# An encoder block in three stages: one program, expert lists of 128 slots, lists made on ScalarE, and another order of ScalarE's step

## The chip, the cores and the metric

The kernel runs on one core of one Trainium2 chip. The metric is the device time of one execution in microseconds, given as the median of several. The change is measured against the kernel before in the same way.

## The reference, cut to what matters

The block takes 512 rows (tokens) of 1024 float32 values:

```python
h = layer_norm(x)
# mixing: projections, spatial gating, stick-breaking attention, two gated branches
merged = sigmoid(gate_a) * (yA @ w_branch_a) + sigmoid(gate_b) * (yB @ w_branch_b)
h = layer_norm(ALPHA * h + merged @ w_out)
# experts: sigmoid scores, 4 of 8 groups, 8 of 64 experts per token
r = ALPHA * h + sum over the 8 picked experts e of
        weight[e] * ((silu(h @ gate[e]) * (h @ up[e])) @ down[e])      # 1024 -> 256 -> 1024
      + (silu(h @ sh_gate) * (h @ sh_up)) @ sh_down                    # one shared expert
r = r + sigmoid(r @ ple_w_gate) * (p @ ple_w_proj)
out = layer_norm(r)
```

Each of the 64 experts sees 64 tokens in the mean (512 x 8 / 64). The weights of one expert are 3 MB: gate, up and down with 1 MB each.

## The kernel before

It is written instruction by instruction, with semaphores. Every float32 product is made of three products of parts: an operand is split into a high part (ScalarE rounds it to the type fp32r) and a low part (VectorE subtracts the high part from the whole), and `product3` (L400 to L402) multiplies high by high, low by high and high by low.

Three functions, each with a Block of its own, follow each other; between two Blocks all engines meet. `mix_block` makes everything up to the merged rows. `out_block` multiplies them with `w_out` (weight pieces 22 to 25 of a ring with two raw buffers and four split ones), normalises the rows, stores them to `h1`, turns them, and begins the shared expert (`gate_up(0)`). `experts_block` makes the router's scores (`score`, `turn_scores`), picks the experts (`pick`, `weigh`), gives each pair of token and expert a slot in the expert's list (`count`, `place`), finishes the shared expert (`gate_up`, `turn_h`, `down`, `add_rows`, `store_rows`), and runs a loop over the 64 experts. At last `Embedding` makes the per-layer input and the last norm.

A list has `SLOTS` = 96 places. No expert has more tokens here, so one round over the experts is enough; a second would run if one had more. `one_hot` compares the slot numbers (`slots`, laid out by one iota in 16 groups of 6) with the tokens' slots (L1663); `locate` multiplies that with tags (L1480); `find` sums them to token number and weight, and makes the list for the gather (L1671, L1676). An unused place gets a number beyond the last token, and the transfer skips it. GpSimd gathers the rows from `h1` by an indirect transfer (`gather`, L1791) and adds the results to one of two tensors in memory, even and odd experts apart (`scatter`, L1803, an indirect transfer with addition).

In the loop, the step of expert x is written out for each engine:

- SyncE: load down(x); load gate and up of x+2, each as soon as VectorE has made the low part that frees its buffer.
- TensorE: turn the hidden rows of x-1 (L1513), locate x+4, gate and up of x (24 matmuls), turn the gathered rows of x+1 (L1489, 8 matmuls), down of x-1 (12 matmuls).
- ScalarE: high part of the hidden rows of x-1 (L1599); high parts of gate and up of x+1 (L1580); silu of x (L1595); high part of the gathered rows of x+1 (L1590); high part of down x (L1586); scaling of the result rows of x-1 (L1605).
- VectorE: low part of the hidden rows of x-1 (L1709); low part of gate of x+1 (L1688); find x+4; one-hot x+5; low part of up of x+1; product with up (L1704); low part of the gathered rows of x+1 (L1698); low part of down x (L1693); list for the scatter of x (`put_list`, L1682, two buffers).
- GpSimd: gather x+4, scatter x-1.

Of the kernel before, what the change touches and what calls it, by code (L numbers as in the profile page):

```python
# [12 lines left out]

# [3 lines left out]
P = 128  # L17
# [15 lines left out]
SLOTS = 96  # L33
FAR = 4096.0
QUEUES = 16
# [13 lines left out]
KB = 1024  # L49


class Memory:


    def __init__(self, nc, base, cap):
# [48 lines left out]
        self.peak_i = at("peak_i", [P, 1], I32, 206)  # L104

# [24 lines left out]
        self.put_idx = [at(f"put_idx{i}", [P, 1], U32, 180.75 + i * 0.0625) for i in range(2)]  # L130
# [11 lines left out]
        self.hT_lo = at("hT_lo", [P, 2, 2 * cap], F32R, 181)  # L142
        self.y = [at(f"y{i}", [P, D], F32, 102 + 4 * i) for i in range(2)]
        self.onehot = at("onehot", [P, 2, NT, cap], BF16, 182.5)
# [10 lines left out]
def set_constants(nc, m, pool, base_set, constants_set, cap):  # L155
# [8 lines left out]
    pool.wait_ge(base_set, 7)  # L164
    for eye in (m.ident, m.ident_bf):
# [12 lines left out]
    nc.gpsimd.iota(m.slots[:, 0:rounds * cap].rearrange("p (r q j) -> p r q j", r=rounds, q=QUEUES),  # L178
                   pattern=[[cap, rounds], [1, QUEUES], [QUEUES, cap // QUEUES]], base=0, channel_multiplier=0,
                   allow_small_or_imprecise_dtypes=True)  # L180
# [306 lines left out]
def mix_block(nc, m, ps, norm_semaphores, a, h0, ring, merged_turn, CAP):  # L487
# [8 lines left out]
    with ExitStack() as ctx:  # L496
        def sem(name):
            return ctx.enter_context(nc.semaphore(f"mix_{name}"))

        half_used, projected, gelu_out, copied = sem("half_used"), sem("projected"), sem("gelu_out"), sem("copied")  # L500
        small_in = sem("small_in")
        sg_turned, sg_w_ready = sem("sg_turned"), sem("sg_w_ready")
        v_moments, v_rooted = sem("v_moments"), sem("v_rooted")
        v_stats, v_scaled, v_normed = sem("v_stats"), sem("v_scaled"), sem("v_normed")
        gated, ya_ready = sem("gated"), sem("ya_ready")
        ya_turned, ya_hi, ya_lo = sem("ya_turned"), sem("ya_hi"), sem("ya_lo")
        z_ready, sig_ready, a_ready = sem("z_ready"), sem("sig_ready"), sem("a_ready")
        a_turned, aT_ready, av_done = sem("a_turned"), sem("aT_ready"), sem("av_done")
        yb_hi, yb_lo = sem("yb_hi"), sem("yb_lo")
        gate_sum, branch_sum, gate_ready, merged = sem("gate_sum"), sem("branch_sum"), sem("gate_ready"), sem("merged")  # L510
        chain, base_set, constants_set = sem("chain"), sem("base_set"), sem("constants_set")
        norm = RowNorm(nc, m, ps, norm_semaphores, banks=(3, 5))
        for c in range(5):
            ring.freed[2 * c], ring.freed[2 * c + 1] = (half_used, c + 1), (projected, 4 * c + 4)
        for j in range(4):
            ring.freed[10 + 3 * j] = (half_used, 5 + j + 1)
            ring.freed[11 + 3 * j], ring.freed[12 + 3 * j] = (gate_sum, 4 * j + 4), (branch_sum, 4 * j + 4)
        block = ctx.enter_context(nc.Block())
# [3 lines left out]
        SPLIT_AFTER_PAIR = {6: (14,), 7: (15,), 8: (16,), 14: (17,), 15: (18, 19)}  # L522
        SPLIT_AFTER_GATE = {10: (20,), 11: (21,), 12: (22,)}

        LAST_BEFORE_H0 = DENSE_PIECES - 6

        def width(s):
            return (s // HEADS + 1) * P

        def block_done(p):  # L530

            qb, last = divmod(p - 3, 4)
            return qb if p >= 3 and last == 3 else None

        def unit_bank(u):
            return FIRST_UNITS[u] if u < len(FIRST_UNITS) else MAIN[u % 2]

        @block.sync
        def _(sp):
            def load_rows(t):  # L540
                sp.dma_start(m.x[:, t], a["x"][0][t * P:(t + 1) * P, :]).then_inc(norm_semaphores.rows_in[t], 16)

            load_rows(0)
            norm.load_affine(sp, a["ln_in_g"], a["ln_in_b"])
            load_rows(1)
            ring.load(sp, 0)
            ring.load(sp, 1)
            load_rows(2)
            load_rows(3)
            sp.dma_start(m.sg_w[:], a["sg_w_s"][0].rearrange("g i j -> i g j")).then_inc(small_in, 16)  # L550
            norm.store(sp, 0, h0)
            norm.store(sp, 1, h0)
            ring.load(sp, 2)
            ring.load(sp, 3)
            sp.dma_start(m.sg_g[:], a["sg_ln_g"][0].partition_broadcast(P)).then_inc(small_in, 16)
            sp.dma_start(m.sg_bb[:], a["sg_ln_b"][0].partition_broadcast(P)).then_inc(small_in, 16)
            sp.dma_start(m.sg_b[:], a["sg_b_s"][0].rearrange("g i -> i g"),
                         allow_slow_non_contiguous=True).then_inc(small_in, 16)
            norm.store(sp, 2, h0)
            norm.store(sp, 3, h0)  # L560
            for i in range(4, DENSE_PIECES):
                ring.load(sp, i)
                if i == LAST_BEFORE_H0:
                    norm.stored(sp)
                    sp.wait_ge(branch_sum, 8)
                    for t in range(NT):
                        sp.dma_start(m.x[:, t], h0[t * P:(t + 1) * P, :]).then_inc(merged_turn.rows_in, 16)

        @block.gpsimd
        def _(pool):  # L570
            set_constants(nc, m, pool, base_set, constants_set, CAP)

        @block.tensor
        def _(pe):
            def unit_start(u):

                if u < 4:
                    return
                if u < 6:
                    pe.wait_ge(gelu_out, u - 3)  # L580
                elif u - 2 >= 8:
                    pe.wait_ge(copied, u - 2 - 8 + 1)
                else:
                    pe.wait_ge(gelu_out, u - 2 + 1)

            def rows_unit(u, c, t, between=None):

                unit_start(u)
                for half in range(2):
                    i = 2 * c + half  # L590
                    if t == 0:
                        ring.ready(pe, i)
                    for k in range(4):
                        kk = 4 * half + k
                        last = product3(nc, ps[:, unit_bank(u)], m.act_hi[:, kk, t * P:(t + 1) * P],
                                        m.act_lo[:, kk, t * P:(t + 1) * P], ring.hi(i)[:, k], ring.lo(i)[:, k],
                                        kk == 0, kk == KD - 1)
                    if half == 0 and t == NT - 1:
                        last.then_inc(half_used, 1)
                    if half == 0 and between is not None:  # L600
                        norm.turn(pe, between)
                last.then_inc(projected, 1)

            def features_unit(u, c, f):

                unit_start(u)
# [64 lines left out]
            def gate_part(g, part):  # L671
# [18 lines left out]
                if part < 3:  # L690
                    return
# [1391 lines left out]
```

## Time and profile before

| | us |
|---|---|
| median of 3 runs | 1160.66 |
| lowest, highest | 1159.36, 1161.66 |
| the profiled execution | 1162.54 |
| its span, first to last instruction | 1160.7 |

A reader of the rows below should know: PE is TensorE's matmuls, PEld its weight loads, DVE is VectorE, ACT is ScalarE, POOL is GpSimd and SP is SyncE. A row of a stretch has the start and end, its length, busy us of PE, PEld, DVE, ACT and POOL with the number of instructions, the granted clock as a share of full speed, the mean share of the 16 transfer engines that was busy, and what they moved. A group has a line, an engine, an operation, output and inputs with shapes and its count; then busy time in us and mean ns of one, then idle time before it and what ended that. Since matmuls overlap, the start of one to the start of the next is their pace, not their duration.

### The profile page before, as it was taken

What the parts mean: (1) busy time and instruction counts of PE and PEld (TensorE: products, weight loads), DVE (VectorE), ACT (ScalarE), POOL (GpSimd) and SP (SyncE); (2) the same over time, 40 slices, a digit from 0 to 9 for tenths busy, and PEclk for the clock granted to TensorE, in tenths of its full rate; (3) what the DMA queues carried; (4) which work ended last, traced back from release to release, by engine and by line L of the source; (5) the groups of instructions that cost most, each with busy time, mean ns of one, the idle gap of its engine ahead of it and who ended that gap; (6) DMA issues with size and microseconds to landing.
All of it is one profiled execution on the core that took longest, in us unless ns stands there. A gap on an engine that the chain in (4) does not pass through costs nothing.

```text
span 1160.7 us, 15673 instructions
## 1 busy us (share of the span) xinstructions
PE 1098.8 (95%) x5374; PEld 821.6 (71%) x5374; DVE 842.4 (73%) x1030; ACT 682.2 (59%) x689; POOL 316.6 (27%) x179
## 2 busy tenths in 40 slices
PE   4999999999999889999999999999999999999796
PEld 3878776668878557777777776767777777677475
DVE  6644437453356567999999988989889989887376
ACT  3332325351223326888888878778778878777253
POOL 1000000000004423444444434424334433231431
PEclk9999999989999899999999999999999999999898
DMA  8522213023256357999999999999999999997821
GB/s 316 179 76 73 88 58 109 1 83 121 87 191 235 127 215 257 355 368 370 371 370 363 369 361 368 364 356 363 360 363 365 368 362 364 361 355 248 272 91 55
DMA packets 68477, 294.79 MB, mean 254 GB/s; under 512 B 11217, under 2 KB 14289, under 8 KB 43601
## 3 DMA queue, kind: packets, MB, share of 16 engines
q1 hardware_dynamic: 52944, 256.43, 58.6%
q0 software_dynamic: 14912, 35.68, 12.5%
q10 hardware_dynamic: 576, 2.10, 0.5%
q8 instruction: 27, 0.44, 0.2%
q14 instruction: 18, 0.14, 0.0%
HBM read 275.29 MB, written 35.65 MB: 268 GB/s over the span
## 4 chain that ended last, share of the span: by engine, by line
PE 40%; DMA 14%; DVE 6%; issue 3%; ACT 3%; ACTq 0%; DVEq 0%; SPq 0%
PE ps L400 11%; PE ps L402 11%; PE ps L401 11%; DMA gu_raw<-in_moe_w_up 10%; DMA gu_raw<-in_moe_w_gate 4%; PE ps L1489 3%; ACT w_hi L1580 2%; DVE w_lo L1688 2%; PE ps L1943 1%; PE ps L1229 1%; PE ps L1513 1%; PE ps L1480 1%; DVE w_lo L384 1%; DVE grp L1297 0%; PE ps L1924 0%
## 5 line engine op out<-in xcount | busy, mean ns | idle before, releaser
L1688 DVE TENSOR_TENSOR w_lo<-gu_raw,w_hi 128x2048 fp32r<-128x2048 f32 x126 | 288.4, 2290 | 53.1 <-ACT w_hi L1580 53.0
L1580 ACT ACTIVATE w_hi<-gu_raw 128x2048 fp32r<-128x2048 f32 x128 | 242.6, 1913 | 52.7 <-DMA gu_raw<-in_moe_w_up 39.5
L400 PE MATMUL ps<-w_hi,xgT_hi 128*96 128x512 f32 x512 | 205.8, 402 | 5.7 <-issue 3.2
L1791 POOL DMA_INDIRECT xg<-h_rows,get_idx x64 | 154.3, 2410 | 204.9 <-DVE get_idx L1676 162.2
L402 PE MATMUL ps<-w_hi,xgT_lo 128*96 128x512 f32 x512 | 203.1, 397 | 0.0
L401 PE MATMUL ps<-w_lo,xgT_hi 128*96 128x512 f32 x512 | 201.6, 394 | 0.0
L400 PE MATMUL ps<-w_hi,act_hi 128*128 128x512 f32 x384 | 154.9, 404 | 6.1 <-PEq L496 2.8
L402 PE MATMUL ps<-w_hi,act_lo 128*128 128x512 f32 x384 | 150.9, 393 | 0.0
L401 PE MATMUL ps<-w_lo,act_hi 128*128 128x512 f32 x384 | 150.9, 393 | 0.0
L1693 DVE TENSOR_TENSOR dn_lo<-dn_raw,dn_hi 128x2048 fp32r<-128x2048 f32 x64 | 146.1, 2283 | 5.5 <-ACT dn_hi L1586 5.0
L1586 ACT ACTIVATE dn_hi<-dn_raw 128x2048 fp32r<-128x2048 f32 x64 | 122.2, 1910 | 12.9 <-issue 8.5
L279 POOL TENSOR_TENSOR x_rows<-x_rows,ln_b 128x1024 f32<-128x1024 f32 x6 | 14.4, 2394 | 384.1 <-DVE x_rows L272 384.1
L400 PEld LDWEIGHTS ps<-w_hi,xgT_hi 128*96 128x96 f32 x512 | 83.0, 162 | 39.3 <-issue 5.3
L402 PEld LDWEIGHTS ps<-w_hi,xgT_lo 128*96 128x96 f32 x512 | 82.9, 162 | 36.2
L400 PE MATMUL ps<-dn_hi,hT_hi 128*96 128x512 f32 x256 | 105.2, 411 | 1.9 <-DVE hT_lo L1709 1.9
L401 PEld LDWEIGHTS ps<-w_lo,xgT_hi 128*96 128x96 f32 x512 | 83.2, 162 | 32.2
L402 PE MATMUL ps<-dn_hi,hT_lo 128*96 128x512 f32 x256 | 101.7, 397 | 0.0
L401 PE MATMUL ps<-dn_lo,hT_hi 128*96 128x512 f32 x256 | 101.1, 395 | 0.0
L379 ACT ACTIVATE w_hi<-raw 128x2048 fp32r<-128x2048 f32 x28 | 53.3, 1913 | 63.4 <-PE ps L402 48.1
L400 PEld LDWEIGHTS ps<-w_hi,act_hi 128*128 128x128 f32 x384 | 73.0, 190 | 22.7 <-DVE act_lo L482 3.0
L402 PEld LDWEIGHTS ps<-w_hi,act_lo 128*128 128x128 f32 x384 | 72.9, 190 | 15.8
L384 DVE TENSOR_TENSOR w_lo<-raw,w_hi 128x2048 fp32r<-128x2048 f32 x27 | 61.4, 2288 | 30.5 <-ACT w_hi L379 30.4
(200 smaller groups left out, 1679.1 us busy)
## 6 DMA issues: line engine op xcount, KB each, us to landing
gu_raw<-in_moe_w_gate SPq DMA_DIRECT2D x64, 1024.0 KB, 15.0
gu_raw<-in_moe_w_up SPq DMA_DIRECT2D x64, 1024.0 KB, 14.6
dn_raw<-in_moe_w_down SPq DMA_DIRECT2D x64, 1024.0 KB, 14.7
raw<-in_w_in SPq DMA_DIRECT2D x18, 1024.0 KB, 5.1
h_rows<-x_rows SPq DMA_DIRECT2D x8, 512.0 KB, 5.1
raw<-in_w_out SPq DMA_DIRECT2D x4, 1024.0 KB, 5.5
ple_raw<-in_ple_w_gate SPq DMA_DIRECT2D x4, 1024.0 KB, 9.7
x_rows<-in_x SPq DMA_DIRECT2D x4, 512.0 KB, 9.7
```

The lines of the kernel that those rows point to most:

```text
L279: self.nc.gpsimd.tensor_tensor(m.x[:, t], m.x[:, t], m.ln_b[:], ALU.add).then_inc(self.s.normed, 1)
L379: self.nc.scalar.activation(self.m.w_hi[:, i % NSPLIT], self.raw[i % self.slots], ACT.Copy).then_inc(self.hi_split, 1)
L384: (unit or self.nc.vector).tensor_tensor(self.m.w_lo[:, i % NSPLIT], self.raw[i % self.slots], self.m.w_hi[:, i % NSPLIT].bitcast(F32), AL ...
L400: nc.tensor.matmul(out, x_hi, w_hi, start=first, stop=False)
L401: nc.tensor.matmul(out, x_hi, w_lo, start=False, stop=False)
L402: return nc.tensor.matmul(out, x_lo, w_hi, start=False, stop=last)
L1489: last = nc.tensor.transpose(ps[:, XT + k // 4, (k % 4) * CAP:(k % 4 + 1) * CAP], m.xg[x.q][0:CAP, k::KD], m.ident[0:CAP, 0:CAP])
L1580: nc.scalar.activation(m.w_hi[:, 2 * x.b + half], m.gu_raw[:, 2 * x.b + half], ACT.Copy).then_inc(gu_hi, 1)
L1586: nc.scalar.activation(m.dn_hi[:, x.b], m.dn_raw[:, x.b], ACT.Copy).then_inc(dn_hi, 1)
L1688: nc.vector.tensor_tensor(m.w_lo[:, 2 * x.b + half], m.gu_raw[:, 2 * x.b + half], m.w_hi[:, 2 * x.b + half].bitcast(F32), ALU.subtract).th ...
L1693: nc.vector.tensor_tensor(m.dn_lo[:, x.b], m.dn_raw[:, x.b], m.dn_hi[:, x.b].bitcast(F32), ALU.subtract).then_inc(dn_lo, 1)
L1791: nc.gpsimd.indirect_dma_start(out=m.xg[x.q][0:CAP], out_offset=None, in_=h1, in_offset=bass.IndirectOffsetOnAxis(ap=m.get_idx[x.q][0:CAP] ...
```

## The change

The three functions become stages (`mix_stage`, `out_stage`, `experts_stage`) whose parts for each engine run one after the other in a single Block, so no engine waits for the others between them; waits that the boundaries stood for are now on semaphores of their own. Around the old boundaries work is placed anew: piece 24 of the weights is split in the first stage; GpSimd's low parts (piece 27 and expert 0) go to VectorE; two shared gate-and-up products stand ahead of the scores instead of one; of the four shared down products two stand ahead of the first `locate`; and the order of VectorE's and ScalarE's work there follows it.

A list has 128 slots. The slot numbers are laid out by two iotas in another order. The list for the scatter is made by ScalarE from four buffers, and in ScalarE's step the scaling of x-2 and the list of x stand between the high parts of gate and up of x+1.

```diff
-SLOTS = 96
+SLOTS = 128
-QUEUES = 16
...
-    nc.gpsimd.iota(m.slots[:, 0:rounds * cap].rearrange("p (r q j) -> p r q j", r=rounds, q=QUEUES),
-                   pattern=[[cap, rounds], [1, QUEUES], [QUEUES, cap // QUEUES]], base=0, channel_multiplier=0,
+    parts = m.slots[:, 0:rounds * cap].rearrange("p (r h u g v) -> p r h u g v", r=rounds, h=2, u=2, g=8)
+    for u in range(2):
+        nc.gpsimd.iota(parts[:, :, :, u], pattern=[[cap, rounds], [8, 2], [1, 8], [32, 4]], base=16 * u,
```

The end of the first stage, ScalarE and then VectorE:

```diff
+        ring.split_hi(act, 24)
             merged_turn.high_part(act, 1)
...
+        ring.split_lo(dve, 24)
             merged_turn.low_part(dve, 1)
```

The second stage, SyncE:

```diff
-            norm.load_affine(sp, a["ln1_g"][0], a["ln1_b"][0])
             routing.load_router(sp)
+        sp.wait_ge(*ring.freed[FIRST - 1])
+        norm.load_affine(sp, a["ln1_g"][0], a["ln1_b"][0])
             early.load_gate_up(sp, Expert(0, 0, 0))
             ring.load(sp, FIRST + 4)
+        ring.load(sp, FIRST + 5)
             sp.wait_ge(merged_turn.lo_done, NT)
             early.load_gate_up(sp, Expert(0, 0, 1))
-            ring.load(sp, FIRST + 5)
             for t in range(NT):
+            if t == NT - 1:
+                sp.wait_ge(ring.lo_split, FIRST + 5)
+                routing.load_down(sp)
                 norm.store(sp, t, h1)
-            norm.stored(sp)
```

The second stage, TensorE:

```diff
-            pe.wait_ge(norm_semaphores.lo_done, norm.before + 1)
+        pe.wait_ge(norm_semaphores.lo_done, norm.before + 2)
             routing.gate_up(pe, 0)
             norm.turn(pe, NT - 1)
+        routing.gate_up(pe, 1)
+        pe.wait_ge(norm_semaphores.lo_done, norm.before + NT)
```

The experts, TensorE ahead of the loop:

```diff
             routing.score(pe)
+        routing.gate_up(pe, 2, halves=(0,))
             routing.turn_scores(pe)
-            routing.gate_up(pe, 1)
-            routing.gate_up(pe, 2)
-            routing.count(pe)
+        routing.gate_up(pe, 2, halves=(1,))
             routing.gate_up(pe, 3)
-            locate(Expert(0, 0, 0))
-            locate(Expert(0, 0, 1))
             routing.turn_h(pe, 0)
             routing.turn_h(pe, 1)
+        routing.down(pe, 0)
+        routing.count(pe)
+        routing.down(pe, 1)
+        locate(Expert(0, 0, 0))
+        routing.turn_h(pe, 2)
+        locate(Expert(0, 0, 1))
+        routing.turn_h(pe, 3)
+        routing.down(pe, 2)
             locate(Expert(0, 0, 2))
+        routing.down(pe, 3)
             locate(Expert(0, 0, 3))
-            for t in (0, 1):
-                routing.down(pe, t)
-                routing.turn_h(pe, t + 2)
-            pe.wait_ge(routing.hT_ready, NT)
             turn_x(Expert(0, 0, 0))
-            routing.down(pe, 2)
-            routing.down(pe, 3)
             rounds(pe, body)
```

The experts, ScalarE:

```diff
+        def put_list(x, at=99):
+
+            if at not in (0, 2):
+                act.wait_ge(put[x.b], 16 * (x.turn2 - 2 + ZEROS[x.b]))
+            act.wait_ge(found, x.it + 1 + LEAD)
+            nc.scalar.activation(m.put_idx[x.q][0:CAP],
+                                 m.found[0:CAP, bass.ds(x.e, 1), 0:1].rearrange("p o c -> p (o c)"),
+                                 ACT.Identity, bias=m.far[0:CAP]).then_inc(put_ready, 1)
...
                     if at not in (0, -1):
                         split(x.next(1), 0)
+                if at not in (0, 1):
+                    scale_y(x.next(-2))
+                put_list(x, at if first else 99)
+                if at not in (0, -1):
                         split(x.next(1), 1)
...
                     if at != 0:
                         split_down(x)
-                    if at != 0:
+                if at == -1:
                         scale_y(x.next(-1))
```

The experts, VectorE ahead of the loop:

```diff
+        split(Expert(0, 0, 0), 0)
             routing.times_up(dve, 0)
+        split(Expert(0, 0, 0), 1)
+        routing.times_up(dve, 1)
             routing.copy_logits(dve)
             routing.pick(dve)
+        routing.times_up(dve, 2)
+        routing.times_up(dve, 3)
             routing.weigh(dve)
             routing.place(dve)
```

The experts, GpSimd ahead of the loop:

```diff
+        pool.wait_ge(*routing.rows_stored)
             gather(Expert(0, 0, 0), clear=2)
```

## Rows read from the trace of the kernel before

**Rows 1.** View of transfers: DMA share by slices, the gathers' queue, their issues.
```profile
DMA  8522213023256357999999999999999999997821
...
q0 software_dynamic: 14912, 35.68, 12.5%
...
xg<-h_rows,get_idx POOLq DMA_INDIRECT x64, 9.7
```

**Rows 2.** Stretch of the experts by engine, clock, DMA share and GB/s.
```profile
441.70:1075.50 633.80, 621.11 (x3128) 455.91 (x3128) 563.46 (x618) 498.47 (x440) 248.49 (x122) 1.00 1.00 354
```

**Rows 3.** The chain in order of time: start, us, what.
```profile
656.92 16.04 DMA gu_raw<-in_moe_w_up
672.98 1.93 ACT w_hi L1580
674.93 2.31 DVE w_lo L1688
```

**Rows 4.** Timeline of PE, turns of gathered rows: start, us, what.
```profile
440.61 1.02 PE L1489 MATMUL ps<-ident,xg 96*128 96x96 f32 x8
...
458.83 1.03 PE L1489 MATMUL ps<-ident,xg 96*128 96x96 f32 x8
...
468.46 1.03 PE L1489 MATMUL ps<-ident,xg 96*128 96x96 f32 x8
...
1061.10 1.03 PE L1489 MATMUL ps<-ident,xg 96*128 96x96 f32 x8
```

**Rows 5.** Timeline of POOL around two experts, and three stretches there.
```profile
707.01 2.86 POOL L1791 DMA_INDIRECT xg<-h_rows,get_idx  x1 [2.77 <-DVE get_idx L1676]
713.75 1.45 POOL L1803 DMA_INDIRECT residual_rows<-y,put_idx  x1 [3.88 <-ACT y L1605]
...
713.00:715.50 2.50, 2.50 (x12) 1.78 (x11) 1.70 (x4) 2.12 (x3) 1.45 (x1) 1.00 1.05 333
715.50:718.30 2.80, 2.80 (x18) 2.21 (x17) 2.61 (x5) 2.04 (x2) 0.00 (x0) 1.00 0.98 386
718.60:720.40 1.80, 1.80 (x10) 1.23 (x9) 1.80 (x2) 1.80 (x2) 1.80 (x1) 1.00 1.08 305
```

**Rows 6.** Timeline of PE around the first boundary.
```profile
320.92 1.04 PE L472 MATMUL ps<-ident,merged 128*128 128x128 f32 x8
324.75 0.47 PE L400 MATMUL ps<-w_hi,act_hi 128*128 128x512 f32 x1 [2.79 <-PEq L496]
...
337.37 0.82 PE L472 MATMUL ps<-ident,merged 128*128 128x128 f32 x6
```

**Rows 7.** Timeline of PE and DVE around the second boundary and the routing.
```profile
381.30 1.13 PE L309 MATMUL ps<-ident,x_rows 128*128 128x128 f32 x8 [0.79 <-DVE act_lo L321]
...
385.51 0.66 PE L400 MATMUL ps<-act_hi,r_hi 128*64 128x512 f32 x1 [3.08 <-PEq L1011]
...
395.12 0.43 DVE L1291 TENSOR_TENSOR sel<-score,r_bias 128x256 f32<-128x256 f32 x1 [0.97 <-ACT score L1248]
...
413.24 1.02 DVE L1663 TENSOR_TENSOR onehot<-slots,slot_of 128x384 bf16<-128x384 f32 x2
...
434.99 0.45 PE L400 MATMUL ps<-w_hi,xgT_hi 128*96 128x512 f32 x1
```

**Rows 8.** Groups at 580 to 1000 us, then of the whole span by form.
```profile
L1688 DVE TENSOR_TENSOR w_lo<-gu_raw,w_hi 128x2048 fp32r<-128x2048 f32 x83 | 190.1, 2291 | 37.8 <-ACT w_hi L1580 37.7
...
L1698 DVE TENSOR_TENSOR xgT_lo<-ps,xgT_hi 128x768 fp32r<-128x768 f32 x41 | 38.8, 947 | 0.3 <-ACT xgT_hi L1590 0.3
...
L1590 ACT ACTIVATE xgT_hi<-ps 128x768 fp32r<-128x768 f32 x41 | 33.2, 809 | 11.9 <-PE ps L1489 11.8
...
L482 DVE TENSOR_TENSOR act_lo<-ps,act_hi 128x1024 fp32r<-128x1024 f32 x4 | 4.9, 1222 | 1.0 <-ACT act_hi L478 1.0
...
L185 ACT ACTIVATE rstd<-mv,eps 128x1 f32<-128x1 f32 x16 | 4.3, 289 | 13.0 <-DVE mv L247 12.9
...
L478 ACT ACTIVATE act_hi<-ps 128x1024 fp32r<-128x1024 f32 x4 | 4.1, 1020 | 20.6 <-PE ps L472 20.6
```

More of the change, by code:

```diff
@@ L12 @@
 from contextlib import ExitStack
+from dataclasses import dataclass
 import concourse.bass as bass
@@ L49 @@
 KB = 1024
+@dataclass
+class Stage:
+    sync: object
+    tensor: object
+    scalar: object
+    vector: object
+    gpsimd: object
+    prime: object = None
 class Memory:
@@ new lines, in rows_unit, with features_unit @@
+                if half == 0 and between is not None:
+                    norm.turn(pe, between)
+            last.then_inc(projected, 1)
+        def features_unit(u, c, f):
+            unit_start(u)
+            for half in range(2):
+                i = 2 * c + half
+                if f == 0:
+                    ring.ready(pe, i)
+                cols = slice(f * P, (f + 1) * P)
+                for k in range(4):
+                    kk = 4 * half + k
+                    last = product3(nc, ps[:, MAIN[u % 2]], ring.hi(i)[:, k, cols], ring.lo(i)[:, k, cols],
+                                    m.act_hi[:, kk], m.act_lo[:, kk], kk == 0, kk == KD - 1)
+                if half == 0 and f == 3:
+                    last.then_inc(half_used, 1)
+            last.then_inc(projected, 1)
@@ new lines, in tensor @@
+        pe.wait_ge(constants_set, 1)
+        norm.turn(pe, 0)
+        norm.turn(pe, 1)
+        for t, between in enumerate((None, 2, 3, None)):
+            pe.wait_ge(norm_semaphores.lo_done, t + 1)
+            rows_unit(t, 0, t, between)
+        pe.wait_ge(small_in, 64)
+        for g in range(SGG):
+            last = nc.tensor.transpose(ps[:, SGT, g * P:(g + 1) * P], m.sg_w[:, g], m.ident[:])
+        last.then_inc(sg_turned, 1)
+        for t in range(NT):
+            rows_unit(4 + t, 1, t)
@@ new lines, in tensor @@
+        for p in range(NPAIRS + 1):
+            if p < NPAIRS:
+                scores(p)
+            for part in (2 * p, 2 * p + 1):
+                gate_part(part // 4, part % 4)
+            if p >= 2:
+                weighted_values(p - 2)
+            if p >= 1:
+                turn(2 * p - 2)
+                turn(2 * p - 1)
+        gate_part(8, 2)
+        weighted_values(NPAIRS - 1)
+        gate_part(8, 3)
+        for g in range(9, 16):
+            for part in range(4):
+                gate_part(g, part)
+            if g >= 14:
+                pe.wait_ge(merged, g - 1)
+                merged_turn.turn(pe, g - 14)
@@ L1117 @@
 class Routing:
-    LOGIT, SCORE, MAIN, POS, ALL = 0, 3, (5, 2, 1, 0), 6, 7
-    TURN, SUM = (4, 3), (5, 1)
+    LOGIT, SCORE, MAIN, POS = 0, 3, (5, 6, 1, 2), 7
+    TURN, SUM = (4, 0), (5, 1)
+    ALL = slice(NT * NE, (NT + 1) * NE)
     GU_PIECE = DENSE_PIECES
```

1833 lines of the change are left out of this document (892 added, 941 removed).

## The prediction

> **What bounds the kernel now.** I read the page first, then the stretches, the chain, and last the lines of one expert.
>
> The view of transfers shows the DMA engines full from slice 17 to 35, the gathers and scatters on a queue of their own, and a gather landing 9.7 us after its issue [rows 1]. The stretch of the experts, from the first turned hidden rows to the last product, holds 633.8 us, over half of the time: PE 98% busy, DVE 89%, ACT 79%, the DMA engines' share 1.00 [rows 2]. Two of these could set the pace, so the chain decides. Its pieces in the middle of that stretch are a transfer of 16 us, the high part 1.9, the low part 2.3, and the next transfer into the buffer just freed [rows 3]: nothing waits there for an engine, all wait for transfers. Where PE isn't held up, two turns of gathered rows follow each other in 9.63 us (458.83 to 468.46). From the second turn to the last (440.61 to 1061.10) it is 620.5 us for 62 experts, 10.01 us each [rows 4]. So PE's floor is 9.63 and the transfers make 10.0 of it; the queue ahead is used up first, and the rest is paid in the later two thirds.
>
> Why are the transfers slow? The stretches of 2 to 3 us around one expert differ [rows 5]. The gather issued at 707.01 lands about 9.7 us later, so its rows move at 713 to 716: 333 GB/s there. Just behind, with loads of weights alone, it is 386. The scatter issued at 713.75 follows, and 305 is what moves then. The engines' share is near 1 in all of them. A gather costs more than its bytes: the loads beside it slow down.
>
> Ahead of the experts the path is serial. PE stands 2.79 us at the first boundary, and 3.08 us with the routing still ahead at the second [rows 6, 7].
>
> **The change, part by part.**
>
> *First boundary.* The last weight piece but one (24) is split before the merged rows' second high part, and no barrier stands before the output product. Before, the turn at 320.92 ended at about 322.0 and the product began at 324.75; two products of 24 matmuls each brought PE to the next turn at 337.37, 12.6 us, since matmuls came 0.43 us apart at half clock for the first 3.4 us. At 0.23 us (as the pace in [rows 4], which has 36 matmuls in 9.63 us beside 1.3 us of turns) 48 of them take 11.1. New end 322.0 + 11.1 = 333.1: 4.3 us gained. The split of piece 25 is the last to come; its load goes out at 320 in either kernel and I put its low part at 329.7, when 12 of the second product's 24 matmuls are due (330.0). Were it late, it would cost its own lateness.
>
> *Second boundary.* Now the second shared gate-and-up product (24 x 0.23 = 5.5 us) runs while the last rows' high and low parts are made, where PE stood before. VectorE takes the low part that GpSimd made (2.29 us more on it), and its own row pass is no longer beside GpSimd's; I leave that at nothing. Turn of the last rows 381.3 - 4.3 = 377.0, over at 377.8, product to 383.3, scores 5.5 at full clock to 388.8, half a product 2.8, four small turns and a sigmoid 0.9: the picking starts at 392.5 instead of 395.12, 2.6 us earlier. Picking, weighing and placing keep their 18.1 us (395.12 to 413.24 [rows 7]), plus two products of 0.4 us now within: slots are known at about 411.4.
>
> *Behind the slots.* Before, all four shared down products (16 fp32 matmuls, 13.8 us) lay between the slots and the first expert's product at 434.99 [rows 7]: 21.75 us. Now two of them come before. What is left: one-hot 0.6, locate 0.3, turn and locate 1, two down products 7, two locates 0.6, waits of the locates and add_rows 1.5, the turn 0.8, high part 1.0 and low part 1.2 of the gathered rows: 14.3. The first expert starts at about 425.5, 9.5 us sooner. The third expert's transfers follow the first's splits, so they shift with it. I take -9.5, with 5 and 13 as bounds (nothing gained behind the slots but the boundaries' 2.6 plus half; or all waits gone).
>
> *128 slots on the engines.* Moving operands of the products stay 512 wide. Turned rows: 128 x 128 is what the turns of 320.92 have, 1.04 us for 8 against 1.02 to 1.03 [rows 4, 6]: nothing. VectorE: the low part of gathered rows goes from 768 to 1024 elements, 947 ns to 1222 [rows 8]: +0.27. At that 1.07 ns an element, the one-hot from 384 to 512 adds 0.14; the hidden rows' low part (64 elements more) +0.07. The list moves off: -0.14. Sum +0.34 us an expert, on a VectorE that is busy 563.5/64 = 8.80 us [rows 2]: 9.14, under 9.63. ScalarE: 809 to 1020 ns [rows 8], hidden rows +0.05, the list with a bias operand 0.29 (as the 128x1 activation with bias [rows 8]): +0.55 on 498.5/64 = 7.79 us: 8.34. Both are hidden by the transfers, or by PE if that cover goes; without cover the VectorE part would be 0.34 x 62 = 21 us.
>
> *Order on ScalarE.* Scaling (1.1 us) no longer stands before the next step's high parts. VectorE waited 37.8 us in 420 for these, 0.9 us an expert [rows 8]; the first half of it comes about 1 us sooner, which pays for the +0.34. Queued behind the scaling are now the list and the second high part; VectorE needs the latter only after low part, find and one-hot (3.2 us), and it is there after 1.1 + 0.3 + 1.9 = 3.3. The down product that waits for the scaled rows' bank comes 3 us later still. The scatter leaves later, beside the next gather on GpSimd's queue; its rows are next wanted two steps on, and it lands in about 9 us. Four list buffers take the wait for the last scatter away. Nothing of this shortens the path while transfers bound it.
>
> *The slots' order and the transfers.* The order of `slots` changes with the count. Before, 96 rows are dealt in 16 runs of 6 partitions; now the positions are grouped by 64, 32 and 4. If transfer engine and partition then match as they do for the loads, a gather no longer disturbs them. What that is worth: 2.5 us of gather per expert at 333 instead of 386 GB/s, 2.5 x (1 - 333/386) = 0.34 us as the upper bound, 0 as the lower. Nearest are the loads alone in [rows 5]; a gather reads 4 KB pieces, so I take 0.26. Against it: 32 more empty slots in each list. The 14912 packets of the queue [rows 1] are 64 x 64 rows gathered and as many scattered (512 tokens x 8), 512 of zeros, 16 completions for each of 132 transfers (2112), and 4096 others, which is just (64 x 96 - 4096) x 2: an empty slot makes a small packet. There will be 4096 more, 256 an engine. Between 0 and the queue's mean (12.5% of 16 x 1160.7 us over 14912 = 156 ns, so 40 us in all) I take 15 ns, as whole rows set that mean: 0.06 us an expert. Net -0.2 us: 62 x 0.2 = 12.5 us. The pace comes to 9.8, still above PE's 9.63.
>
> For this case the Trainium skill ("DMA: Bandwidth & Descriptors", The descriptor swizzle) says that in a transfer of 128 partitions the engine is 8 x (p >> 6) + ((p >> 2) & 7), each writing one port; with it the new order gives each engine every sixteenth token on its own port, and the old runs of six crossed ports. By that rule the whole 0.34 would be won and the gain be 5 us larger; no row here shows ports.
>
> **Sum.** -9.5 - 12.5 = -22. The profiled execution has 1162.5 us (span 1160.7), the three times have a median of 1160.66, 1.9 below it. 1162.5 - 22 = 1140.5 for such an execution, and 1.9 less for the median: 1139.
>
> **Rivals.**
> Transfers gain nothing: the gathers are slow because of what they read, or the memory is at its ceiling. For: 4 KB reads from scattered rows, a share near 1 in every stretch. Against: 386 GB/s without gathers. Then -9.5 + 62 x 0.06 = -6, less what noise adds: 1151 to 1155. The Trainium skill has on the same page (Specifications) a memory limit of about 358 GB/s per core, by which no layout would help; the 386 of [rows 5] is against it.
> PE sets the pace from end to end: a relief of the full 0.34 and free empty slots give 62 x 0.34 = 21, with -9.5: 1130. [rows 4] show that the engines can go at 9.63, but experts' tokens differ, and so the demand varies about its mean.
> VectorE becomes the bound: its 9.14 us busy with the 0.9 of waits kept beside it make a step of over 10.0, and it decides from 10.17 on (9.5 us over 62 more than 10.01). At 10.5 the time is 1160.7 - 9.5 + 62 x 0.5 = 1182, slower. Against it: the waits come from late transfers, and ScalarE's new order takes the first away.
> The boundaries gain little since a down product or gather is waited for instead: with the transfers unrelieved, 1158 to 1162.
>
> **How the numbers follow.** The forecast (partial relief) 0.52, PE-bound 0.15, no relief 0.24, boundaries and relief both nearly nothing 0.04, VectorE-bound 0.05. Prediction 1139; from the PE-bound case to the middle of no relief: 1126 to 1153. What can be told from no change is about 0.2%, 2.3 us: faster 0.91, same 0.04, slower 0.05.
>
> **What would show it.** Right: the first expert's product at about 425; gather stretches above 350 GB/s; turns 9.8 us apart; low parts of gathered rows at 1.22 us with DVE under 95% busy. Wrong: turns still 10.0 apart with gather stretches near 330 (no relief); PE waiting for low parts while VectorE has no idle (VectorE-bound); the first product later than 431 (boundaries); GpSimd's gathers longer than 4 us, which would make its queue late.

## The result, and the profile after

| | before | after |
|---|---|---|
| median, us | 1160.01 (4 runs) | 1122.56 (4 runs) |
| lowest to highest, us | 1157.49 to 1161.66 | 1120.06 to 1123.35 |
| span of the profiled execution, us | 1160.7 | 1121.4 |
| ratio, 95% interval | | 0.967 (0.965 to 0.970) |

The kernel is faster by 37.5 us. The forecast was a gain of 22 and a time of 1139, in a range from 1126 to 1153, so the measured time lies 3.4 us below the range.

The page of the kernel after has these lines on the slices' DMA share, the gathers' queue and the shares of the chain:

```profile
DMA  9432222114365357999999999999999999997911
...
q0 software_dynamic: 19008, 35.71, 12.5%
...
PE 88%; DVE 6%; DMA 2%; issue 2%; ACT 1%; SPq 0%; DVEq 0%; POOLq 0%; ACTq 0%
```

The page of the kernel before has these shares of the chain:

```profile
PE 40%; DMA 14%; DVE 6%; issue 3%; ACT 3%; ACTq 0%; DVEq 0%; SPq 0%
```

The transfers' share is as high as before [rows 1], but the chain now goes through PE, where its pieces in the middle were transfers and splits [rows 3]. The extra packets are the 4096 that were forecast. Four stretches of the kernel after (columns as in [rows 2]): the experts, a gather, what follows it, and a scatter:

```profile
430.00:1040.00 610.00, 606.02 (x3134) 510.72 (x3132) 583.70 (x553) 524.37 (x502) 264.50 (x122) 1.00 1.00 370
...
711.60:715.20 3.60, 3.60 (x21) 3.13 (x21) 3.56 (x5) 2.63 (x4) 2.06 (x2) 1.00 1.01 420
715.30:717.50 2.20, 2.20 (x11) 1.82 (x10) 2.20 (x3) 2.20 (x2) 2.08 (x1) 1.00 1.01 425
717.50:720.50 3.00, 3.00 (x19) 2.51 (x18) 2.83 (x3) 2.83 (x4) 0.00 (x0) 1.00 1.02 325
```

Where a gather's rows move, it is 420 GB/s against 333 [rows 5]; behind it 425 against 386; in the scatter 325 against 305. A share of 1.00 says only that the engines have packets in hand, not how fast these move.

The marks on PE of the kernel after, to be set beside [rows 4, 6, 7]:

```profile
317.69 1.04 PE L486 MATMUL ps<-ident,merged 128*128 128x128 f32 x8
...
329.94 0.27 PE L486 MATMUL ps<-ident,merged 128*128 128x128 f32 x1
...
373.18 1.02 PE L323 MATMUL ps<-ident,x_rows 128*128 128x128 f32 x7 [0.42 <-DVE act_lo L335]
...
418.97 0.47 PE L414 MATMUL ps<-w_hi,xgT_hi 128*128 128x512 f32 x1 [2.34 <-issue]
...
426.16 1.04 PE L1504 MATMUL ps<-ident,xg 128*128 128x128 f32 x8
...
1021.30 0.93 PE L1504 MATMUL ps<-ident,xg 128*128 128x128 f32 x7
```

And on VectorE, from the picking to the one-hot:

```profile
388.86 0.42 DVE L1310 TENSOR_TENSOR sel<-score,r_bias 128x256 f32<-128x256 f32 x1 [2.84 <-ACT score L1267]
391.63 0.22 DVE L1316 TENSOR_TENSOR grp<-top 128x32 f32<-128x32 f32 x1
...
404.11 1.29 DVE L1690 TENSOR_TENSOR onehot<-slots,slot_of 128x512 bf16<-128x512 f32 x2
```

Worked out from these marks, the 39.3 us between the two spans are:

| stretch | before | after | difference |
|---|---|---|---|
| to the second turn of the merged rows (not part of the change) | 320.92 | 317.69 | -3.23 |
| on to the next turn (first boundary) | 16.45 | 12.25 | -4.20 |
| on to the last turn of rows | 43.93 | 43.24 | -0.69 |
| on to the picking (second boundary) | 13.82 | 15.68 | +1.86 |
| picking to one-hot | 18.12 | 15.25 | -2.87 |
| one-hot to the first expert's product | 21.75 | 14.86 | -6.89 |
| on to the second turn of gathered rows | 5.62 | 7.19 | +1.57 |
| 62 experts | 620.49 | 595.14 | -25.35 |
| the rest | 99.6 | 100.1 | +0.5 |

The first row is chance: the same stretch of the first stage runs at full clock in one execution and at part of it in another. Here are the 8 us from 236 on in the kernel before and in the kernel after:

```profile
236.00:244.00 8.00, 6.39 (x32) 4.22 (x33) 2.11 (x4) 3.08 (x4) 0.00 (x0) 0.57 0.01 2
```

```profile
236.00:244.00 8.00, 6.90 (x46) 5.23 (x47) 3.41 (x4) 5.18 (x8) 0.00 (x0) 1.00 0.01 2
```

Granted clock 0.57 and 1.00, so part of the stretch at 1.2 GHz and all of it at 2.4 GHz. Over all profiles, the second turn of the merged rows lies at 320.92, 318.36, 320.32 and 317.35 in the four with the old program, and from 317.00 to 321.29 in the nine with the new one. It follows the clock of these 8 us and not the program: 317.0 to 317.7 at a clock of 1.00, 318.2 to 318.7 at 0.79, 320.3 to 321.3 at 0.57.

The +1.57 is the clock's too (0.50 from 419.7 to 423.1), but it isn't chance of that kind. The four profiles of the old program have 5.55 to 5.62 us there. Of the nine of the new one, six have 7.1 to 8.2, and in them the clock falls to half in or just behind a stand of PE of 2.34 us ahead of the first expert's product; three have 5.5 to 5.6, with a stand of 1.65 to 2.12 us there and full clock. So this is a cost of the new front that most profiled executions pay.

### The profile page after: what moved, and what is told of

It reads as the page before. It is cut to its first block, busy times and chain, and to the rows that moved or that the text cites. A ratio compares the mean times of both kernels' runs of the same rounds, so it can differ in the third digit from the quotient of the medians.

```text
span 1121.4 us, 15663 instructions
## 1 busy us (share of the span) xinstructions
PE 1071.5 (96%) x5374; PEld 871.5 (78%) x5374; DVE 865.8 (77%) x969; ACT 709.8 (63%) x753; POOL 315.1 (28%) x178
## 3 DMA queue, kind: packets, MB, share of 16 engines
q0 software_dynamic: 19008, 35.71, 12.5%
## 4 chain that ended last, share of the span: by engine, by line
PE 88%; DVE 6%; DMA 2%; issue 2%; ACT 1%; SPq 0%; DVEq 0%; POOLq 0%; ACTq 0%
PE ps L414 26%; PE ps L416 25%; PE ps L415 24%; PE ps L1504 5%; DVE w_lo L398 2%; PE ps L1954 1%; PE ps L1528 1%; PE ps L729 1%; PE ps L753 1%; PE ps L740 1%; ACT w_hi L393 1%; DMA xg<-h_rows,get_idx 1%; DMA ln_b<-in_ln_in_b 1%; DMA raw<-in_w_out 1%; DVE stick L995 0%
## 5 line engine op out<-in xcount | busy, mean ns | idle before, releaser
L414 PE MATMUL ps<-w_hi,xgT_hi 128*128 128x512 f32 x512 | 206.6, 403 | 4.9 <-issue 4.8
L416 PE MATMUL ps<-w_hi,xgT_lo 128*128 128x512 f32 x512 | 201.6, 394 | 0.0
L415 PE MATMUL ps<-w_lo,xgT_hi 128*128 128x512 f32 x512 | 200.9, 392 | 0.0
L414 PEld LDWEIGHTS ps<-w_hi,xgT_hi 128*128 128x128 f32 x512 | 96.8, 189 | 24.1 <-issue 5.3
L416 PEld LDWEIGHTS ps<-w_hi,xgT_lo 128*128 128x128 f32 x512 | 96.9, 189 | 20.9
L415 PEld LDWEIGHTS ps<-w_lo,xgT_hi 128*128 128x128 f32 x512 | 97.0, 189 | 18.5
L414 PE MATMUL ps<-dn_hi,hT_hi 128*128 128x512 f32 x256 | 105.4, 412 | 2.0 <-DVE hT_lo L1730 2.0
L416 PE MATMUL ps<-dn_hi,hT_lo 128*128 128x512 f32 x256 | 101.0, 395 | 0.0
L415 PE MATMUL ps<-dn_lo,hT_hi 128*128 128x512 f32 x256 | 100.2, 391 | 0.0
L1604 ACT ACTIVATE xgT_hi<-ps 128x1024 fp32r<-128x1024 f32 x64 | 65.7, 1027 | 41.0 <-PE ps L1504 41.0
```

Of the source, the lines that this page charges most:

```text
L414: nc.tensor.matmul(out, x_hi, w_hi, start=first, stop=False)
L415: nc.tensor.matmul(out, x_hi, w_lo, start=False, stop=False)
L416: return nc.tensor.matmul(out, x_lo, w_hi, start=False, stop=last)
L1604: nc.scalar.activation(m.xgT_hi[:, x.b].rearrange("p (c n) -> p c n", c=2), x_banks(), ACT.Copy).then_inc(x_hi, 1)
```

## The experiments

All times are medians; "pace" is the mean us of an expert from the second turn of gathered rows to the last, over 62 experts. The kernel before had medians of 1162.5, 1161.7 and 1162.9 us beside the three groups of runs, and each ratio is to the kernel before of its own group. PE's floor is its pace where nothing holds it up: most steps of the kernel after take 9.52 to 9.55 us, which the text calls 9.53. First the whole, then each kernel:

| kernel | us | ratio to before, 95% | pace |
|---|---|---|---|
| before | 1160.0 | | 10.01 |
| before, 128 slots in the new order | 1175.9 | 1.005 to 1.016 | 10.24 |
| the same, four lists | 1152.1 | 0.991 to 0.995 | 9.91 |
| the same, scaling between the high parts | 1135.7 | 0.973 to 0.980 | 9.59 |
| after | 1122.6 | 0.965 to 0.970 | 9.60 |
| after, 96 slots in the old order | 1153.8 | 0.990 to 0.995 | 10.12 |
| after, 128 slots in 16 runs | 1216.8 | 1.042 to 1.049 | 11.08 |
| after, ScalarE's old order | 1150.6 | 0.988 to 0.994 | 9.99 |
| after, list on VectorE | 1122.4 | 0.961 to 0.967 | 9.59 |
| after, half a one-hot more | 1137.1 | 0.977 to 0.985 | 9.80 |
| after, low parts on GpSimd | 1122.8 | 0.962 to 0.968 | 9.57 |
| the same, one beside the picking | 1121.2 | 0.962 to 0.969 | 9.59 |
| after, slots in bf16 | 1123.9 | 0.964 to 0.969 | 9.57 |

**128 slots alone.**

```diff
-SLOTS = 96
+SLOTS = 128
-    nc.gpsimd.iota(... pattern=[[cap, rounds], [1, QUEUES], [QUEUES, cap // QUEUES]] ...)
+    for u in range(2):
+        nc.gpsimd.iota(parts[:, :, :, u], pattern=[[cap, rounds], [8, 2], [1, 8], [32, 4]], base=16 * u, ...)
```

> The kernel before with 128 slots and the new order of the slot numbers, and nothing else (hidden rows' low part and one-hot moved in SBUF to make room). Theory A, the form and order of the lists relieve the transfers: the loop's pace falls from 10.01 to about 9.65 us an expert, 62 x 0.36 = 22, so about 1138, with the first expert's product still near 435. Theory B, ScalarE's order and the list on ScalarE bring the loop's gain: the pace stays at 10.0 or rises by the small packets and VectorE's 0.34 us, so 1160 to 1165.

Neither theory came true: it is 16 us slower than the kernel before (13 by the runs beside it), though the transfers were relieved. A gather's stretch, then waits of 560 to 980 (us in total, times, longest), then pieces of the chain:

```profile
702.20:705.50 3.30, 3.30 (x18) 2.79 (x17) 2.58 (x3) 2.09 (x3) 0.91 (x1) 1.00 1.01 422
```

```profile
DVE put_idx L1683 <- DMA odd_rows<-y,put_idx: 12.1, 12, 1.8
...
DVE w_lo L1689 <- ACT w_hi L1581: 3.4, 9, 0.6
```

```profile
606.20 13.48 DMA odd_rows<-y,put_idx
619.80 0.11 DVE put_idx L1683
...
627.38 12.84 DMA odd_rows<-y,put_idx
```

ScalarE doesn't wait for weights any more, and VectorE hardly for ScalarE (3.4 us where [rows 8] have 37.7). Instead VectorE stands before `put_list`: with two list buffers it may write the list of x only when the scatter of x-2 has landed, and a scatter takes 13 us here. Behind that wait stand the low parts of the next expert.

**The same with four lists.**

```diff
-    self.put_idx = [at(f"put_idx{i}", ...) for i in range(2)]
+    self.put_idx = [at(f"put_idx{i}", ...) for i in range(4)]
...
-                dve.wait_ge(put[x.b], 16 * (x.turn2 - 1 + ZEROS[x.b]))
+                if at not in (0, 2):
+                    dve.wait_ge(put[x.b], 16 * (x.turn2 - 2 + ZEROS[x.b]))
```

> The kernel before with 128 slots, the new order of the numbers, and four buffers for the scatter's list (still made by VectorE at the end of its step). Its likeness with two buffers took 1176, with VectorE waiting 19 us in 420 for scatters. Theory E, that wait is what kept the relief of the transfers from showing: it goes, the pace falls from 10.24 to 9.7 or less, so 1140 to 1145. Rival, the scatter's ring through ScalarE's scaling and GpSimd's queue holds it as well: 1160 or above.

24 us less than with two lists, and the pace falls from 10.24 to 9.91: that wait held the relief back in the first kernel. It wasn't all: 9.91 is still far from PE's floor of 9.53.

**The same with the scaling moved.**

```diff
                     split(x.next(1), 0)
+                if at not in (0, 1):
+                    scale_y(x.next(-2))
                     split(x.next(1), 1)
...
-                if at != 0:
+                if at == -1:
                     scale_y(x.next(-1))
```

> The kernel before, its three programs and boundaries kept, with 128 slots, the new order of the numbers, four lists on VectorE, and the scaling of x-2 between the two high parts on ScalarE. Only the scaling's place differs from the kernel with four lists that took 1152 at a pace of 9.91. Theory D, the scaling's place takes 1.1 us out of the ring of two steps: the pace goes to 9.60 to 9.70, and with the old front (first turn of the loop at 439.5 in place of 427) the time is 1135 to 1141. Rival, the list on VectorE keeps the ring long: 9.8 and above, 1147 or more.

As theory D has it: 1135.7, pace 9.59. This loop equals that of the kernel after but for the engine that makes the list. In the same group of runs the kernel after with its list on VectorE took 1122.4, so the front alone is 13.4 us (second turn of gathered rows 438.87 here, 425.53 there); some 1.3 of them are a first boundary that is longer here than in the kernel before, 17.7 us against 16.45.

**After with 96 slots in the old order.**

> The changed kernel (one program, new order on ScalarE, list on ScalarE) with lists of 96 slots in the old order of numbers. Theory A: only the 14.5 us ahead of the loop stay, the pace goes back to 10.0, so 1122.6 + 24 = about 1146. Theory B: the loop keeps its 9.6, about 1122, or less by VectorE's shorter operations.

8 us above theory A: the pace is 10.12, not 10.0. A gather, what follows it, and waits of 560 to 980:

```profile
698.60:703.00 4.40, 4.40 (x19) 3.14 (x20) 4.40 (x4) 2.91 (x3) 0.77 (x1) 1.00 1.02 333
703.20:706.00 2.80, 2.80 (x18) 2.22 (x17) 1.49 (x3) 2.78 (x3) 2.05 (x2) 1.00 1.02 398
```

```profile
ACT w_hi L1594 <- DMA gu_raw<-in_moe_w_up: 48.1, 36, 2.0
DVE w_lo L1709 <- ACT w_hi L1594: 41.0, 39, 1.9
```

333 GB/s again, and weights are waited for again. The front's gain of 15.5 us (second turn at 425.06 against 440.61) has shrunk to 8.6 at the last turn (1052.51 against 1061.10). From the third turn on a step takes 9.64 us, up to the 18th; then the queue ahead is used up and the transfers set the end.

**After with 128 slots dealt in 16 runs.**

> The changed kernel with 128 slots, but the numbers dealt as before, in 16 runs, of 8 places now. If only the whole-height transfer of 128 rows matters: as the changed kernel, 1122 to 1125. If the match of place and transfer engine matters: the filled places of a list lie in half of each group of 16 places, so the rows of a gather fall on few engines, its stretches fall below 350 GB/s again, and the pace goes to 9.9 or more: 1140 or above.

Far slower, over 90 us above the kernel after. A gather and the stretch behind it:

```profile
699.10:702.70 3.60, 3.60 (x22) 3.10 (x21) 2.12 (x5) 2.62 (x3) 2.51 (x2) 1.00 0.99 356
703.00:705.00 2.00, 2.00 (x11) 1.63 (x10) 2.00 (x3) 2.00 (x2) 0.00 (x0) 1.00 0.95 309
```

So 128 places without the new order are worse than 96 with the old: among lists of 128, what counts is that an expert's some 64 rows fall evenly on the engines. By the Trainium skill ("DMA: Bandwidth & Descriptors", The descriptor swizzle) four neighbouring partitions belong to one engine, and 64 rows in runs of 8 places, half of each filled, fall on 8 of the 16 engines; that fits the time, while the rows here name no engine. The packets of the traces bear it out by their times alone. From 560 to 980 more than 8 packets of a scatter were under way at once for 46 us in the kernel after and for 8 us here, and fewer than 16 packets of all kinds for 9 us there and for 90 us here.

**After with ScalarE's old order**, the scaling of x-1 and then the list at the end of the step:

```diff
                     split(x.next(1), 0)
-                if at not in (0, 1):
-                    scale_y(x.next(-2))
-                put_list(x, at if first else 99)
-                if at not in (0, -1):
                     split(x.next(1), 1)
...
-                if at == -1:
+                if at != 0:
                     scale_y(x.next(-1))
+                put_list(x, at if first else 99)
```

> The changed kernel with ScalarE's old order in a step: the list and the scaling of x-1 at the end, ahead of both high parts of the next step. Theory D, with fast transfers the order is what lets PE set the pace (the scatter's 11 to 13 us and the scaling stand in a ring with the next high part): the pace rises from 9.60 to 9.9 or more, so 1140 or above. Rival, the order is worth nothing once lists have four buffers and stand on ScalarE: 1122 to 1126.

28 us slower than after. Its chain around 740 to 760, from one low part of gathered rows to that two steps on:

```profile
740.15 1.15 DVE xgT_lo L1716
...
741.42 0.49 PE ps L414
...
748.99 1.89 ACT dn_hi L1600
...
752.06 0.28 ACT put_idx L1620
752.34 0.28 ACT hT_hi L1613
752.62 1.81 ACT w_hi L1594
...
757.57 2.29 DVE w_lo L1706
759.86 0.33 DVE h_ff L1722
760.19 1.14 DVE xgT_lo L1716
```

A ring of two steps, 20.04 us, so 10.02 a step: low part of x's rows, gate and up of x with the turn behind them, high part of down, scaling, list, high part of the hidden rows, high part of the next expert's first half, its low parts. Scaling and list hold it for 1.4 us (750.9 to 752.34). Without them it would be some 18.6, 9.3 a step, and PE's 9.53 is longer.

**After with the list on VectorE.** `put_list` stands at the end of VectorE's step, with four buffers.

> The changed kernel with the scatter's list made by VectorE at the end of its step, from four buffers. VectorE's load is 9.12 + 0.09 to 0.15 us a step. The half one-hot of 0.42 us raised the pace by 0.20, so cover is about 0.2: the list should be hidden for the most part, pace 9.60 to 9.66, 1122 to 1127. Rival, the list's move to ScalarE is a main part of the gain: 1130 or above.

No difference: 1122.4, pace 9.59. Four buffers and the scaling's place count, not the engine that makes the list.

**After with half a one-hot more.**

```diff
 def one_hot(x):
+            nc.vector.tensor_tensor(m.onehot[:, x.b, 0:2], ..., ALU.is_equal).then_inc(half_hot, 1)
+            dve.wait_ge(half_hot, x.it + 1)
             nc.vector.tensor_tensor(m.onehot[:, x.b], ..., ALU.is_equal).then_inc(hot_ready, 1)
```

> The changed kernel with half a one-hot more on VectorE in each step, some 0.4 us (its result is overwritten). VectorE is busy 583.7/64 = 9.12 us of a step of 9.60. Theory F, PE sets the pace and VectorE has cover: up to 0.4 us are hidden in the main, 1123 to 1130. Rival, VectorE's work is in the ring that sets the step: 62 x 0.4 = 25 us, about 1147.

Between the two, so neither holds: some 15 us, pace +0.20 for 0.42 us of work. The 9.12 of the expectation is too low, since its stretch takes in the ends of the loop, where VectorE has less to do. From 440 to 700 the kernel after and this one have

```profile
440.00:700.00 260.00, 260.00 (x1363) 219.81 (x1362) 254.44 (x245) 228.23 (x219) 117.14 (x54) 1.00 1.01 378
```

```profile
440.00:700.00 260.00, 256.86 (x1320) 215.15 (x1319) 256.66 (x266) 222.16 (x212) 129.47 (x53) 1.00 1.01 371
```

VectorE is busy 254.44/260 x 9.60 = 9.39 us a step in the kernel after, 0.21 below its pace. Here it is busy for 98.7% and PE no longer all the time, so VectorE sets the pace. Of the 0.42 us 0.20 were paid and some 0.2 were hidden, which fits the 0.21.

**GpSimd beside VectorE.** In the first kernel GpSimd makes expert 0's low parts, as before the change; in the second the latter of these also waits for the scores (`wait_ge(routing.scored, 1)`, which the first has not).

```diff
+        pool.wait_ge(gu_lo, 2 * LEAD)
+        split(Expert(0, 0, 0), 0)
+        pool.wait_ge(routing.scored, 1)
+        split(Expert(0, 0, 0), 1)
```

> The changed kernel, but the low parts of expert 0's gate and up are made by GpSimd again, beside VectorE's picking. Theory C, GpSimd's subtraction stretches VectorE's operations beside it: the small masks of the picking take 3 to 4 us again where they overlap, the time from the start of the picking to the one-hot goes from 15.25 to about 18, and the kernel is 2 to 4 us slower, about 1125. Rival: the 3.77 us that one mask took before was another wait and doesn't come back: 1121 to 1123, or less, since VectorE has 4.6 us fewer to do.

The time stayed, but it tests nothing: GpSimd was done at 387.3, before the picking began at 389.64.

> As the kernel with expert 0's low parts on GpSimd, but the second starts with the scores, so that its 4.6 us lie beside VectorE's picking. Theory C: the sum of the two best (0.22 us alone) takes 3 to 4 us again, the one-hot comes 3.5 us later, and the kernel takes 1125 to 1127. Rival: it stays 0.22 and the time 1123.

VectorE's sum of the two best, and GpSimd's operation beside it:

```profile
392.14 2.20 DVE L1316 TENSOR_TENSOR grp<-top 128x32 f32<-128x32 f32 x1
```

```profile
389.41 4.85 POOL L1827 TENSOR_TENSOR w_lo<-gu_raw,w_hi 128x2048 fp32r<-128x2048 f32 x1 [6.95 <-ACT score L1267]
```

and in the kernel before the change:

```profile
397.89 3.77 DVE L1297 TENSOR_TENSOR grp<-top 128x32 f32<-128x32 f32 x1
```

```profile
396.98 4.61 POOL L1810 TENSOR_TENSOR w_lo<-gu_raw,w_hi 128x2048 fp32r<-128x2048 f32 x1 [3.21 <-ACT w_hi L1580]
```

The mechanism is shown: the 0.22 us take 2.20, and picking to one-hot goes from 15.25 to 17.20. They aren't the forecast 3 to 4, since GpSimd begins earlier against the sum here than before the change. The median isn't 1125 but 1121.2, within the spread of the runs (the profiled execution took 1125.7, the others 1119.7 to 1121.7); at this size the profile tells more than the median.

**After with slots in bf16**: `slots` and `slot_of` are held as bf16, exact for lists of up to 256 places.

> The changed kernel with the slot numbers and the tokens' slots held as bf16 (exact for lists of up to 256 places), so that the one-hot's comparison reads and writes bf16. If VectorE's 0.69 us falls to 0.45 or less, VectorE is relieved by 0.2 us a step; PE's floor of 9.53 then shows in every step, where now every fourth takes 9.65: 62 x 0.04 = 2.5 us, and some 0.5 ahead of the loop: about 1119 to 1121. Rival, the operation takes as long as before, since its operands are broadcast: 1122 to 1123.

The rival's time is right: the one-hot takes 692 ns with either type. That the broadcast is the reason was not tested.

```profile
L1690 DVE TENSOR_TENSOR onehot<-slots,slot_of 128x512 bf16<-128x512 bf16 x44 | 30.4, 692 | 1.3
```

## Why the prediction was too careful

**First boundary, -4.3.** Measured -4.20, and 12.0 to 12.3 us against 16.4 to 17.7 in the other profiles of the new and the old program. Right.

**Second boundary, 2.6 earlier.** -4.20 - 0.69 + 1.86 = -3.0 without the chance in the first stage. Right.

**"Picking, weighing and placing keep their 18.1 us."** They took 15.25, with the two products within. The prediction thought of GpSimd beside VectorE for the row pass alone and left it at nothing; in the picking it was 3.55 us at one instruction of 0.22 (3.77 in the trace of before). 18.1 + 0.8 - 3.55 is 15.35.

**Behind the slots, 14.3.** Measured 14.86. Right, though its term before was misread: the four down products took 16 us there, part of them at half clock, and not 13.8. The front as a whole gave -12.8 by the marks (-11.2 with the half clock behind the first product), and -13.4 by the kernel with the old front and the new loop, where I had -9.5. The missing 3.3 are the stall of the picking.

**VectorE +0.34, ScalarE +0.55, both hidden.** VectorE's load in the loop went from 234.85/260 x 10.01 = 9.04 to 9.39, +0.35. Hidden, though with 0.21 to spare and not the 0.5 that 9.14 under 9.63 promised, and the sign "DVE under 95% busy" did not hold (97.9% from 440 to 700). The groups from 560 to 980 agree on the parts and show the waits for ScalarE gone:

```profile
L1709 DVE TENSOR_TENSOR w_lo<-gu_raw,w_hi 128x2048 fp32r<-128x2048 f32 x89 | 203.2, 2283 | 0.7 <-ACT w_hi L1594 0.7
...
L1719 DVE TENSOR_TENSOR xgT_lo<-ps,xgT_hi 128x1024 fp32r<-128x1024 f32 x44 | 53.6, 1217 | 0.0
```

**"Net -0.2 us: 62 x 0.2 = 12.5 us. The pace comes to 9.8."** This is the step that failed: the relief of the transfers and so the pace, which moved by -0.41 to 9.60, 25.4 us. Its upper bound of 0.34 took the 386 GB/s behind a gather, in [rows 5] from 715.5 to 718.3, as what loads alone do. But the gather issued at 707.01 lands at 716.7 by its own 9.7 us, so its last rows are in that stretch, and in the 2.5 us of the bound not all of it is counted. The kernel before, asked in finer stretches, has

```profile
711.00:712.50 1.50, 1.50 (x12) 1.23 (x11) 1.03 (x1) 1.21 (x2) 0.00 (x0) 1.00 1.01 426
713.00:716.50 3.50, 3.50 (x17) 2.44 (x16) 2.70 (x4) 3.12 (x3) 1.45 (x1) 1.00 1.01 334
716.50:718.50 2.00, 2.00 (x14) 1.69 (x13) 1.81 (x5) 1.06 (x3) 0.13 (x1) 1.00 1.05 428
```

Loads alone move 426 to 428 there, and the bound would have been 3.5 x (1 - 334/427) = 0.76 us, more than the 0.38 between 10.01 and PE's 9.63. An expert needs 363 GB/s x 10.01 us = 3.63 MB moved (after: 382 x 9.60 = 3.67), and at PE's floor of 9.53 that is some 383 GB/s. With lists of 96 the transfers gave 357 to 363 over 260 and 300 us, in both kernels that have them; with 128 in the new order they give enough, and PE sets the pace. That was the rival with 0.15 and 1130; with the front's true size it would have been some 1127. The term against the relief, 0.06 us for the small packets, was about right: they take 11 ns each in the traces of before and after, which is 0.04 us an expert.

The rest is PE's floor, which is lower by 0.10 (the pace of 9.60 lies 0.07 above it). Here is one step each of the kernel after with 96 slots and of the kernel after, from the turn of the hidden rows to the next turn of gathered rows:

```profile
564.09 0.36 PE L1528 MATMUL ps<-ident,h_ff 96*128 96x96 f32 x2
...
564.74 0.39 PE L415 MATMUL ps<-w_lo,xgT_hi 128*96 128x512 f32 x1
...
570.08 1.02 PE L1504 MATMUL ps<-ident,xg 96*128 96x96 f32 x8
```

```profile
564.77 0.39 PE L1528 MATMUL ps<-ident,h_ff 128*128 128x128 f32 x2
...
565.42 0.39 PE L415 MATMUL ps<-w_lo,xgT_hi 128*128 128x512 f32 x1
...
570.66 1.04 PE L1504 MATMUL ps<-ident,xg 128*128 128x128 f32 x8
```

The gain is not in `locate`, which lies in the first part (0.65 us in both), but in the rest of gate and up (5.34 against 5.24 us); why 23 matmuls with 128 rows take less than with 96 stays open. The weight loads of `locate` do get shorter. Before and after, from 560 to 980:

```profile
L1480 PEld LDWEIGHTS ps<-tags,onehot 128*96 128x96 bf16 x168 | 16.7, 129 | 0.5
```

```profile
L1495 PEld LDWEIGHTS ps<-tags,onehot 128*128 128x128 bf16 x176 | 11.3, 99 | 0.5
```

More columns load in less time. The Trainium skill ("TensorE: Matmul & The Clock Gate", Weight-path perf modes) says that the fast weight load is on when there are 128 weights and the type isn't FP32; the trace agrees. These 4 x 0.03 us overlap with matmuls, and the step does not show them.

**ScalarE's order: "pays for the +0.34", "nothing of this shortens the path while transfers bound it".** True in the main under its condition: 96 slots with the new order have no gain in pace. But the condition fell. Of the loop's gain no part comes near it alone: with the slots alone the pace is 10.24, with slots and four lists 9.91, with the new order (and the new front) alone 10.12, with all 9.60. The old order closes a ring through two steps. With 128 slots it takes 9.9 to 10.0 a step although the transfers are relieved (the kernels with 1152.1 and 1150.6 us). With 96 it is shorter: from the third turn to the 25th the kernel before took 9.76 a step, with less than 1 us of waits for transfers in all, where the new order took 9.64 as long as its own queue lasted. So the ring lay below the transfers' 10.0 in the kernel before and was not to be seen, and the longer operations of 128 slots made it the next bound; the wait for two lists came on top as the scatter landed later. The prediction asked what is late next only of VectorE's busy time, not of the rings through it.

**Adding front and loop.** While transfers bound the loop, 15.5 us ahead of it were worth 8.6 at its end; so my sum for a pace of 9.8 claimed too much there. It did no harm, as PE became the bound and the front counts in full (13.4).

What stays open is why a transfer into 96 places is slower. The packets of the traces show what is slower, from 560 to 980. A row of a gather takes 0.16 us in all kernels with 128 places, the one dealt in 16 runs too, and 0.20 and 0.19 in the two with 96. Of the packets of weights, 8 KB each, 19% and 25% take over 0.34 us with 96 places, against 4% in the kernel after. The engines are as evenly filled with 96 places (fewer than 16 packets under way for 6 and 7 us of 420) as in the kernel after (9). So these are two effects: uneven dealing, which the kernel with 16 runs of 8 pays for, and slow packets, which both kernels with 96 places pay for. That 96 places cross ports, as the prediction has it, fits this; no row shows ports, and another order over 96 places was not tried.

## What to carry to other kernels

A bound on a gain must come from a rate that the disturbance can't have touched: check by issue and landing that nothing of the transfer in question is left in the stretch. Where one resource sets the pace, close every ring through two steps and sum it with the new durations: one that lies a few per cent below is the next bound, and a change that relieves the first and lengthens the ring can even lose. In lists of 128, an indirect transfer should spread its filled places, not its places, over the engines.

## What the runs showed of the hardware

VectorE's small sum with two inputs from SBUF, begun while GpSimd's subtraction ran, was not merely slowed: it stood until that ended. The two end at 401.66 and 401.59 in the kernel before, and at 394.34 and 394.26 in the kernel with GpSimd beside the picking, 0.07 and 0.08 us apart. The 32 `max` ahead of it, with one input each, lay wholly beside GpSimd's operation in the latter kernel (389.83 to 392.10) and took 2.27 us, as the 2.28 without it. The Trainium skill ("SBUF — State Buffer", Who interferes with whom) has the two engines share a port pair as an exclusive lock, which such an operation takes against one of GpSimd that reads SBUF; the trace agrees, and read in time it would have given 3.5 us of the front.

With this one core at work 420 to 428 GB/s moved in stretches of 1.5 to 4 us, and 382 over 300 us. In the stretch of a scatter with addition it is 325, so once the gathers are relieved the scatters are the slow part of the transfers. By the packets of the kernel after, a row of 4 KB takes 0.33 us in a scatter with addition and 0.16 in a gather. The 32 more places of 64 lists, gathered and scattered, made 4096 packets more; the small packets take 11 ns each in the mean.
